# Conv states, samples' B and C, and the second shift's rows turned in a few wide flips; a page buffer and a job order changed with them

## The chip, the cores and the metric

One core of one Trainium2 chip runs the whole program. The metric is the device time of one execution in microseconds (us). The kernel before was timed three times. A difference of about 0.5% is the least that such a measurement tells from none.

## The reference, cut to what matters

The program is one layer of a decode step for a prompt of 256 tokens (blocks of 128) and 8 samples of one token each, all in float32:

```
mod = silu(c) @ w_mod + b_mod               # c: 8 samples and 1 prompt; six parts, shift2 among them
h   = rms_norm(x) * (1 + scale1) + shift1
q, k, v, f, z, xBC, dt, gA, gB = split(h @ w_in)
oA  = forgetting attention                  # samples: 2 cached pages of 128 keys and values each
xa  = concat(conv_state, xBC)               # 3 old columns of 3072 channels ahead of the new ones
conv_new = xa[last 3]                       # an output, for the samples and for the prompt
xs, B, C = split(silu(conv4(xa)))
y   = SSD scan of the prompt in 2 chunks of 128; samples: one state update of 32 x 64 x 128 each
x  += gate1 * (merge of both branches @ w_o)
h2  = rms_norm(x) * (1 + scale2) + shift2
x  += gate2 * moe(h2)                       # 16 experts, top 2 inside one of 4 groups
```

conv_new is written row by row of 3072 channels: 3 rows for each of the 8 samples and 3 for the prompt. The samples' B and C are wanted as rows in a scratch array, from which they are spread over partitions. The router's logits and the tokens' rows of h2 both need shift2.

## The kernel before, in words

The kernel is written in hand-placed instructions with semaphores. Channels lie on partitions ("turned" tensors, 128 channels by 264 tokens), weights come from HBM through a ring of six slots of 1 MB, and TensorE (PE) turns tiles with `flip`, a product with the identity (line 1704). One list, `jobs`, gives the order of the work. Every engine walks it and does its own part of each job: PE fills a PSUM bank, ACT or DVE read it out. The seven banks go round in the order of the list, so a job waits until the job seven banks before it has been read.

The jobs that the text names:

- `xbc i` (24 of them) are the channel blocks of xBC. DVE (L1387 to L1395) puts the old columns ahead, copies the last three columns of each sample and of the prompt into `tails[:, i, 27]`, and sums the convolution. ACT applies SiLU (L924, L925) into `u`.
- `sk b q` turn the samples' key pages, `ss` multiplies queries by keys (L1862 to L1870) and ends in the semaphore `ss_done`, `sm` and `sp` are the softmax and its turning (L1012, L1013 on ACT).
- `so h` (L1888) multiplies probabilities and value pages of samples 4h to 4h+3, `sx h` turns the result and DVE copies it into `att_T` (L1412, 8 copies).
- POOL issues the page loads (L798), key pages first, into the four page buffers `kvr`. For value pages of samples 4 to 7 it waits until `so 0` has left those buffers.
- `ct i`, six jobs, turn `tails` four blocks at a time (27 rows of 512 channels). ACT copies each to SBUF (L1021) and issues two stores (L1022, L1024).
- `bs 0`, `bs 1` turn the samples' columns of the eight B and C blocks (8 flips to 8 rows). ACT copies them (L1027), stores them and the samples' x and decays to scratch (L1031 to L1035) and loads d_skip, spread over partitions (L1036).
- `bt` and `xs a g` turn B and x of the prompt (DVE multiplies xs by dt, L1420), `cb a` is C times B (L1424 masks it), `ab a b` spreads the sums of decays, DVE subtracts (L1439), ACT takes exp (L1049), DVE multiplies by cb (L1222, `weigh`), and `y a b` (L1945, L1948) is the scan's product. POOL scales xs (L805, L812) for the chunk's state and, in the second chunk, C (L823).
- `z i`, 16 jobs of 128 channels, come between these. The list `fill` says where.
- `fs`, the sample states (`ssm`; ACT L1079, DVE L1471 to L1480, loads and stores by POOL L829, L844), the gates `g` and the products `pa` follow, then `yn` (L2026), `sw`, `pb 0` to `pb 7` (L2035), the output product `o` (L2043) and the experts (L2127, L2152, L2181).
- `sw` makes shift2 @ w_router: 8 products with the prompt's column spread over 128 columns, 8 with the samples' 8 columns, and the bias twice (L1965 to L1970). `shr 0` to `shr 3`, after `pb 3`, turn the differences of the samples' shift2 from the prompt's, and the prompt's shift2 itself, one block of 128 channels at a time (16 flips).

SP issues the weights in the order of first use. It waits for the job that last used a slot, and for nothing that is changed here. The loads wait in one queue.

Before its first L1439 DVE waits for the scratch stores and for d_skip, and makes two copies of it (L1434):

```
if a == 0 and b == 0:
    dve.wait_ge(bs_out, 80)
    for q in range(2):
        r = slice(64 * q, 64 * q + 64)
        link(v.tensor_copy(dsk[r, :], dskf[r, q:SH:2]))
```

## Time and profile before

| what | value |
|---|---|
| runs | 774.11, 774.36, 777.66 us; median 774.36 |
| the profiled execution | 773.63 us |
| its span | 772.0 us |
| PE busy | 730.3 us, 95% of the span |
| PEld (weight loads) | 500.8 us, 65% |
| DVE busy | 377.9 us, 49% |
| ACT busy | 291.7 us, 38% |
| POOL busy | 97.8 us, 13% |
| DMA | 219.47 MB, mean 284 GB/s |
| the chain that ended last | 70% PE, 8% DMA, 7% DVE, 6% ACT, 4% issue |

The table is read so. The span is what the profiler saw between the first and the last instruction, and the execution's own time is 1.63 us more. PE, PEld and the others are shares of the span and overlap. An idle PE is what an edit off PE can give back, some 42 us in all. "Issue" in the chain is time in which the engine waited for nothing that the profile shows.

### The profile page before, as it was taken

The numbers are of one execution on the slowest core, as the hardware profiler recorded it, in microseconds if no ns is written. First come the engines' busy times: TensorE is split into PE (matmuls) and PEld (weight loads), VectorE is DVE, ScalarE is ACT, GpSimd is POOL, SyncE is SP. The second block draws the span as 40 slices with busy tenths as digits, with TensorE's granted clock in tenths as the row PEclk, the third lists the DMA queues.
The fourth block names the chain that finished last, engine by engine and source line by source line (L and its number), as shares of the span: only waits on it lengthen the run. The fifth ranks groups of instructions, "written<-read, shape, count | busy, mean of one in ns | idle before, by whom it ended". The sixth has DMA issues, their size and how long they took to land.

```text
span 772.0 us, 12380 instructions
## 1 busy us (share of the span) xinstructions
PE 730.3 (95%) x4469; PEld 500.8 (65%) x4469; DVE 377.9 (49%) x952; ACT 291.7 (38%) x686; POOL 97.8 (13%) x169
## 2 busy tenths in 40 slices
PE   3899998999999989999989999999999999999986
PEld 3475687778785667888877888887634344434433
DVE  1364337777674087587999311112513244324423
ACT  3221157656775223667876001012522122212202
POOL 4331021122110113430111000000010000000000
PEclk9999999999999999999999999999999999999998
DMA  9997374979785621349999797467999999999991
GB/s 313 330 346 226 115 205 153 327 234 321 243 296 176 216 60 60 117 124 367 378 292 336 257 345 272 146 265 294 338 420 422 415 423 422 417 421 421 418 383 60
DMA packets 88649, 219.47 MB, mean 284 GB/s; under 512 B 11990, under 2 KB 55598, under 8 KB 75145
## 3 DMA queue, kind: packets, MB, share of 16 engines
q1 hardware_dynamic: 73360, 181.71, 64.3%
q0 software_dynamic: 7840, 31.67, 12.1%
q10 hardware_dynamic: 7384, 5.25, 2.2%
q8 instruction: 38, 0.62, 0.3%
q14 instruction: 27, 0.21, 0.1%
HBM read 207.07 MB, written 13.22 MB: 285 GB/s over the span
## 4 chain that ended last, share of the span: by engine, by line
PE 70%; DMA 8%; DVE 7%; ACT 6%; issue 4%; SPq 1%; ACTq 1%; POOLq 1%; POOL 0%; DVEq 0%
PE bank L1794 16%; PE bank L2127 13%; PE bank L2035 7%; PE bank L2152 6%; PE bank L2043 4%; PE bank L1704 4%; PE bank L1787 3%; PE bank L2017 3%; DMA conv_out<-in_w_mod 3%; DMA arena<-in_w_up 3%; PE bank L2181 2%; PE bank L1744 2%; DMA arena<-in_state_ssm 2%; DVE arena L1471 1%; ACT arena L1079 1%
## 5 line engine op out<-in xcount | busy, mean ns | idle before, releaser
L1794 PE MATMUL bank<-h_normed,weight_ring 128*128 128x264 f32 x1024 | 237.4, 388 | 2.2 <-ACT conv_work L1087 2.2
L1794 PEld LDWEIGHTS bank<-h_normed,weight_ring 128*128 128x128 f32 x1024 | 191.2, 190 | 37.3 <-issue 4.2
L2127 PE MATMUL bank<-arena,h_normed 128*64 128x512 f32 x136 | 60.3, 594 | 0.0
L2035 PE MATMUL bank<-y_T,weight_ring 128*128 128x264 f32 x256 | 57.4, 386 | 0.4 <-DVE y_T L1508 0.4
L2035 PEld LDWEIGHTS bank<-y_T,weight_ring 128*128 128x128 f32 x256 | 48.5, 190 | 8.7 <-issue 0.5
L1592 DVE TENSOR_TENSOR arena<-arena,bank 128x512 f32<-128x512 f32 x8 | 8.4, 1052 | 85.6 <-PE bank L2127 85.6
L1704 PE MATMUL bank<-identity,arena 128*128 128x128 f32 (+5 forms) x218 | 30.6, 281 | 13.4 <-ACT arena L903 9.5
L1079 ACT ACTIVATE arena<-conv_out,early_small 128x128 f32<-128x128 f32 x128 | 38.3, 387 | 11.3 <-DVE arena L1471 10.2
L2152 PE MATMUL bank<-arena 128*64 128x512 f32 x88 | 39.2, 595 | 0.0
L1395 DVE SCALAR_TENSOR_TENSOR conv_work<-conv_work,conv_out 128x288 f32<-128x288 f32 x72 | 37.8, 525 | 2.5
L872 POOL DMA_INDIRECT h_normed<-h_scratch,token_rows x7 | 7.1, 1018 | 248.7 <-DVE token_rows L1559 135.1
L2127 PE MATMUL bank<-conv_out,h_normed 128*64 128x512 f32 x76 | 34.7, 594 | 2.6 <-DMA arena<-in_w_up 2.5
L1704 PEld LDWEIGHTS bank<-identity,arena 128*128 128x128 f32 (+5 forms) x218 | 26.1, 149 | 17.1 <-issue 11.2
L1133 ACT ACTIVATE h_normed<-bank,conv_tails 128x128 f32<-128x128 f32 x64 | 17.4, 383 | 51.4 <-PE bank L1704 47.9
L2127 PE MATMUL bank<-weight_ring,h_normed 128*64 128x512 f32 x112 | 31.7, 592 | 0.0
L2017 PE MATMUL bank<-att_T,weight_ring 128*128 128x264 f32 x128 | 28.9, 387 | 1.6 <-ACT arena L1085 1.6
L1787 PE MATMUL bank<-h_normed,weight_ring 128*64 128x264 f32 x256 | 29.8, 388 | 0.0
L2043 PE MATMUL bank<-arena,weight_ring 128*128 128x264 f32 x128 | 29.4, 388 | 0.0
L1517 DVE TENSOR_TENSOR arena<-arena,bank 128x264 f32<-128x264 f32 x8 | 3.4, 430 | 51.9 <-PE bank L2035 51.9
L2127 PEld LDWEIGHTS bank<-arena,h_normed 128*64 128x64 f32 x136 | 18.3, 137 | 16.0 <-issue 16.0
L2017 PEld LDWEIGHTS bank<-att_T,weight_ring 128*128 128x128 f32 x128 | 24.2, 190 | 6.1 <-ACT arena L1085 2.0
L1599 DVE SCALAR_TENSOR_TENSOR x_residual<-bank,conv_out,x_residual 128x256 f32<-128x256 f32 x56 | 26.3, 477 | 3.2 <-PE bank L2181 2.7
(407 smaller groups left out, 1227.8 us busy)
## 6 DMA issues: line engine op xcount, KB each, us to landing
weight_ring<-in_w_in SPq DMA_DIRECT2D x36, 1024.0 KB, 6.2
weight_ring<-in_w_mod SPq DMA_DIRECT2D x22, 1024.0 KB, 9.7
arena<-in_w_down SPq DMA_DIRECT2D x11, 1024.0 KB, 23.8
arena<-in_w_gate SPq DMA_DIRECT2D x10, 1024.0 KB, 14.0
weight_ring<-in_w_down SPq DMA_DIRECT2D x10, 1024.0 KB, 14.7
weight_ring<-in_w_up SPq DMA_DIRECT2D x9, 1024.0 KB, 25.0
arena<-in_state_ssm POOLq DMA_DIRECT2D x8, 1024.0 KB, 11.3
out_ssm_sample<-arena POOLq DMA_DIRECT2D x8, 1024.0 KB, 8.8
```

What stands on the lines that cost most here:

```text
L1079: ins = fn(bx[:, NST * c:NST * c + NST], bc[:, b, 0, :], ACT.Copy, scale=xdt[:, c, b:b + 1])
L1133: ins = fn(xg[:, c, :], banks[5 + h][:, 128 * q:128 * q + 128], ACT.Identity, bias=shq[:, c:c + 1])
L1395: link(v.scalar_tensor_tensor(acc, x[:, w:w + XO], vec[:, 104 + 24 * w + i:105 + 24 * w + i], acc, ALU.mult, ALU.add), conv_ready if w == ...
L1599: v.scalar_tensor_tensor(xT[:, c, 0:NP], comb_bank(c)[:, 0:NP], modT[:, 40 + c, NS:NC], xT[:, c, 0:NP], ALU.mult, ALU.add)
L1704: return tr(out, x, ident[0:k, 0:k])
L1787: ins = mm(ps[64 * x:64 * x + 64, 0:T], slot(s)[:, c, o:o + HD], hT[:, c, :], start=c == 0, stop=c == KD - 1, tile_position=(0, 64 * x))
L1794: ins = mm(ps[:, 0:T], w, hT[:, c, :], start=c == 0, stop=c == KD - 1)
L2017: ins = mm(ps[:, 0:T], w, attT[:, c, :], start=c == 0, stop=c == KD - 1)
L2035: ins = mm(ps[:, 0:T], w, yT[:, c, :], start=c == 0, stop=c == NXB - 1)
L2043: ins = mm(ps[:, 0:T], slot(s)[:, c, 128 * (i % 2):128 * (i % 2) + 128], gT[:, c, :], start=c == 0, stop=c == KD - 1)
L2127: ins = mm(banks[i][BLK * e:BLK * e + BLK, :], xg[:, 4 * h + c, BLK * e:BLK * e + BLK], ws[e][c], start=h == 0 and c == 0, stop=h == 1 and ...
L2152: ins = mm(banks[2 + q][BLK * e:BLK * e + BLK, :], aT[:, 2 * h + c, BLK * e:BLK * e + BLK], ws[e][c][:, 512 * q:512 * q + 512], start=h == ...
```

## The change

- The buffer `tails` is laid out as `[128, 6, 27, 4]`: blocks c, c+6, c+12 and c+18 lie beside each other, so that one flip turns 108 columns. `ct` becomes two jobs, of 4 and of 2 flips; four stores take the place of twelve.
- SiLU of the samples' B and C goes to a place of its own (`samples_bc`, 64 columns), which one flip turns: `bs` is one job, put right after `modt 5`.
- The load of d_skip moves to the front of the program (ACT), its copies to DVE's part of `ft`. The router bias gets zeros under it on 128 partitions (one memset on POOL), and its load follows a wait for `consts`. `head_in` counts one load more.
- The value pages of samples 4 to 7 go to a buffer of their own, `kvh`, in the space of the sample queries and turned keys. POOL waits for `ss_done` in place of `so 0`, and PE's `so 1` for the new semaphore `kvh_full`. `so 1` also has its own output buffer.
- `sw` multiplies 72 columns of modT, 16 outputs each, in 8 products and one for the bias. DVE takes the samples' rows and row 8; a job `sb` spreads row 8 over 128 partitions with one product.
- `shr` is one flip of 72 columns, stored to scratch by one DMA. The samples' rows and the prompt's are loaded back from there (two loads in ACT's part of `o 0`), and `rk` waits for these.
- The order between `modt 5` and the scan, and `fill`, are new.

The diff, cut to its core:

```diff
-        tails = sb("conv_tails", [128, NCB, 27])
+        tails = sb("conv_tails", [128, NCB // 4, 27, 4])
...
             if c == 7:
-                jobs += [("sm",), ("mod", 5), ("ct", 0), ("sp",), ("modt", 5)]
+                jobs += [("sm",), ("mod", 5), ("ct", 0), ("sp",), ("modt", 5), ("bs",)]
...
-        jobs += [("so", 0), ("ct", 1), ("sx", 0)] + [("z", i) for i in range(4)] + [("so", 1), ("ct", 2), ("sx", 1)]
-        jobs += [("bs", 0), ("bs", 1)]
-        jobs += [("bt", a) for a in range(2)]
+        jobs += [("z", 0), ("so", 0), ("z", 1), ("sx", 0), ("ct", 1), ("z", 2)] + [("bt", a) for a in range(2)]
+        jobs += [("so", 1), ("z", 3), ("sx", 1)]
         fill = {(0, 1): [("z", 4)], (0, 3): [("z", 5)], 
-                (0, 5): [("z", 6)], (0, 6): [("ct", 3)], (0, 7): [("z", 7)], (1, 0): [("z", 8), ("zs", 0)],
-                (1, 1): [("z", 9)], (1, 2): [("z", 10)], (1, 3): [("z", 11), ("ct", 4), ("zs", 1)], (1, 4): [("z", 12)],
-                (1, 5): [("z", 13), ("zs", 2)], (1, 6): [("z", 14), ("ct", 5)], (1, 7): [("z", 15), ("zs", 3)]}
+                (0, 5): [("z", 6)], (0, 7): [("z", 7)], (1, 0): [("z", 8), ("zs", 0)],
+                (1, 1): [("z", 9)], (1, 2): [("z", 10)], (1, 3): [("z", 11), ("zs", 1)], (1, 4): [("z", 12)],
+                (1, 5): [("z", 13), ("zs", 2)], (1, 6): [("z", 14)], (1, 7): [("z", 15), ("zs", 3)]}
...
-        jobs += [("pb", i) for i in range(4)] + [("shr", i) for i in range(4)] + [("pb", i) for i in range(4, 8)]
+        jobs += [("pb", i) for i in range(4)] + [("shr",), ("sb",)] + [("pb", i) for i in range(4, 8)]
...
-                    if kind == 1 or b >= 4:
-                        bk, use = bank_of[("sk", b - 4, 1) if kind == 0 else ("sk", b + 4, 1) if b < 4 else ("so", 0)]
+                    if kind == 1 and b >= 4:
+                        pool.wait_ge(ss_done, 1)
+                    elif kind == 1 or b >= 4:
+                        bk, use = bank_of[("sk", b - 4, 1) if kind == 0 else ("sk", b + 4, 1)]
                         pool.wait_ge(bank_filled[bk], use)
+                    home = kvh if kind == 1 and b >= 4 else kvr
...
-            act.dma_start(brow[:], t["b_router"].rearrange("(o d) -> o d", o=1)).then_inc(head_in, 16)
+            act.wait_ge(consts, 3)
+            act.dma_start(brow[0:1, :], t["b_router"].rearrange("(o d) -> o d", o=1)).then_inc(head_in, 16)
+            act.dma_start(dskf, t["d_skip"].to_broadcast([128, SH])).then_inc(head_in, 16)
...
-                    link(v.tensor_copy(tails[:, i, 0:24].rearrange("p (b w) -> p b w", w=3), xs4[:, :, 1:4]))
-                    link(v.tensor_copy(tails[:, i, 24:27], x[:, NP:NP + 3]))
+                    tail = tails[:, i % (NCB // 4), :, i // (NCB // 4)]
+                    link(v.tensor_copy(tail[:, 0:24].rearrange("p (b w) -> p b w", w=3), xs4[:, :, 1:4]))
+                    link(v.tensor_copy(tail[:, 24:27], x[:, NP:NP + 3]))
...
                     if a == 0 and b == 0:
-                        dve.wait_ge(bs_out, 80)
-                        for q in range(2):
-                            r = slice(64 * q, 64 * q + 64)
-                            link(v.tensor_copy(dsk[r, :], dskf[r, q:SH:2]))
+                        dve.wait_ge(bs_out, 64)
...
                 elif k == "ct":
                     pe.wait_ge(conv_ready, NCB)
-                    for q in range(4):
-                        ins = flip(ps[0:27, 128 * q:128 * q + 128], tails[:, 4 * j[1] + q, :])
+                    for q in range(4 if j[1] == 0 else 2):
+                        ins = flip(ps[0:4 * 27, 128 * q:128 * q + 128],
+                                   tails[:, 4 * j[1] + q].rearrange("p s q -> p (s q)"))
                 elif k == "bs":
                     pe.wait_ge(u_ready, NCB)
-                    for q in range(4):
-                        ins = flip(ps[0:NS, 128 * q:128 * q + 128], u[:, NXB + 4 * j[1] + q, NP:T])
+                    ins = flip(ps[0:2 * SG * NS, 0:128], samples_bc)
...
                     for c in range(KD):
-                        mm(ps[:, 0:NE], modT[:, 24 + c, NS:NC].to_broadcast([128, 128]), wr[:, c, :],
-                           start=c == 0, stop=False)
-                    mm(ps[:, 0:NE], onesf[0:1, :], brow[:], start=False, stop=True)
-                    for c in range(KD):
-                        mm(ps[0:NS, NE:2 * NE], modT[:, 24 + c, 0:NS], wr[:, c, :], start=c == 0, stop=False)
-                    ins = mm(ps[0:NS, NE:2 * NE], onesf[0:1, 0:NS], brow[:], start=False, stop=True)
+                        mm(ps[0:NC * KD, 0:NE], modT[:, 24 + c:32 + c, :], wr[:, c, :], start=c == 0, stop=False)
+                    ins = mm(ps[0:NC * KD, 0:NE], onesf[:, 0:NC * KD], brow[:], start=False, stop=True)
                 elif k == "shr":
                     pe.wait_ge(shdiff_ready, 1)
-                    for q in range(4):
...
+                    ins = flip(ps[0:NC * KD, 0:128], shifts)
+                elif k == "sb":
+                    read_out(pe, ("sw",))
+                    ins = mm(ps[:, 0:NE], ident[:, NS:NC].to_broadcast([128, 128]), shift9, start=True, stop=True)
...
-                    pe.wait_ge(shdiff_rows, 2)
+                    pe.wait_ge(shq_in, 32)
```

## Rows read from the trace of the kernel before

**Rows 1.** Busy time by stretch: stretch, PE, PEld, DVE, ACT, POOL, PEclk, DMA share, GB/s

```profile
241.50:281.00 39.50, 33.42 (x216) 24.14 (x218) 12.51 (x38) 9.98 (x25) 7.92 (x9) 1.00 0.56 167
281.00:299.70 18.70, 18.70 (x147) 14.95 (x143) 16.63 (x47) 5.80 (x15) 0.00 (x0) 1.00 0.30 90
344.50:403.00 58.50, 57.15 (x290) 49.62 (x288) 52.92 (x62) 47.03 (x121) 8.43 (x16) 1.00 1.03 342
```

**Rows 2.** Timeline of PE, so 0 to the first y: start, length, line, tiles, [idle before]

```profile
244.54 2.92 PE L1888 MATMUL bank<-arena 128*32 128x512 f32 x24 [1.33 <-issue]
...
248.78 14.41 PE L1794 MATMUL bank<-h_normed,weight_ring 128*128 128x264 f32 x64
264.05 2.92 PE L1888 MATMUL bank<-arena 128*32 128x512 f32 x24 [0.87 <-DMA arena<-in_cache_v]
...
268.29 3.66 PE L1704 MATMUL bank<-identity,conv_out 128*8 128x128 f32 x32
...
274.16 0.61 PE L1931 MATMUL bank<-cums_in_parts,head_pick 96*128 96x128 bf16 x8 [1.32 <-ACT arena L1038]
...
280.69 0.66 PE L1945 MATMUL bank<-arena 128*64 128x128 f32 x8 [1.86 <-issue]
```

**Rows 3.** Timeline of DVE, sx 1 to the first weigh

```profile
268.56 1.46 DVE L1412 COPY att_T<-bank 64x8 f32<-64x8 f32 x8 [18.05 <-PE bank L1704]
270.73 2.87 DVE L1420 TENSOR_TENSOR arena<-bank,early_small 128x512 f32<-128x512 f32 x4 [0.71 <-DVE att_T L1412]
...
275.32 2.22 DVE L1434 COPY early_small<-arena 64x16 f32<-64x16 f32 x2 [1.00 <-DMA arena<-in_d_skip]
277.58 2.29 DVE L1439 TENSOR_SCALAR arena<-bank,early_small 128x128 f32<-128x128 f32 x8
279.90 0.69 DVE L1222 TENSOR_TENSOR arena<-arena 128x512 f32<-128x512 f32 x1
```

**Rows 4.** The line of the two copies: ns min/median/max of one, first and last start

```profile
L1434 DVE COPY early_small<-arena x2: 174/1092/2010, 275.3 to 277.4; 64x16 f32<-64x16 f32 x2
```

**Rows 5.** Timeline of POOL, first and last of 8 value pages, then the first scaling

```profile
248.89 0.54 POOL L798 DMA_DIRECT2D arena<-in_cache_v  x1 [19.36 <-issue]
...
259.84 0.54 POOL L798 DMA_DIRECT2D arena<-in_cache_v  x1 [1.33 <-issue]
273.68 3.62 POOL L805 TENSOR_TENSOR arena<-arena,early_small 128x2048 f32<-128x2048 f32 x1 [13.31 <-DVE arena L1420]
```

**Rows 6.** Timeline of all engines, POOL's second scaling and DVE beside it

```profile
305.86 3.62 POOL L812 TENSOR_TENSOR arena<-arena,early_small 128x2048 f32<-128x2048 f32 x1
...
307.87 1.13 DVE L1439 TENSOR_SCALAR arena<-bank,early_small 128x128 f32<-128x128 f32 x4 [1.49 <-ACT arena L1047]
309.03 1.00 DVE L1222 TENSOR_TENSOR arena<-arena 128x512 f32<-128x512 f32 x1
```

**Rows 7.** Timeline of PE, sw and the first pb

```profile
445.07 1.94 PE L1965 MATMUL bank<-conv_out 128*128 128x16 f32 x16
...
448.36 0.91 PE L2035 MATMUL bank<-y_T,weight_ring 128*128 128x264 f32 x3 [0.41 <-DVE y_T L1508]
```

**Rows 8.** The chain that ended last, at shr: start, length, what

```profile
477.08 1.75 PE bank L1704 x16
```

**Rows 9.** The start of the program: PE's timeline, ACT's queue, and the chain

```profile
13.16 4.72 PE L1704 MATMUL bank<-identity,arena 128*128 128x128 f32 x26 [2.70 <-DMA arena<-in_x_sample]
...
33.47 0.66 PE L1704 MATMUL bank<-identity,arena 96*128 96x96 f32 x6
...
13.95 0.30 ACTq L911 DMA_DIRECT2D router_bias<-in_b_router  x1
...
7.33 24.11 DMA conv_out<-in_w_mod
```

**Rows 10.** Waits of PE in the experts: waited for, us in total, times, longest

```profile
PE bank L2127 <- DMA arena<-in_w_up: 2.5, 2, 1.3
```

**Rows 11.** Timeline of PE, gates after a wait, in the stretch of the sample states

```profile
403.84 10.95 PE L1794 MATMUL bank<-h_normed,weight_ring 128*128 128x264 f32 x48 [2.20 <-ACT conv_work L1087]
```

More of the change, by code:

```diff
@@ L113, in build @@
         exo = early[:, 1761:2033]
-        dsk = exo[:, 0:NXB]
+        dskf, dsk = more[:, 0:SH], more[:, SH:SH + NXB]
+        samples_bc = more[:, SH + NXB:SH + NXB + 2 * SG * NS]
         x2, xdt = (exo[:, NXB + 128 * i:NXB + 128 * i + 128].rearrange("p (l b) -> p l b", b=NS) for i in range(2))
@@ L151, in build @@
         pnb = part(NS)
-        bias = [part(768).rearrange("p (h k) -> p h k", h=2),
+        bias_lo = part(768)
+        otoks = (otok, bias_lo[:, 0:KVW])
+        bias = [bias_lo.rearrange("p (h k) -> p h k", h=2),
                 work[:, 0:768].rearrange("p (h k) -> p h k", h=2)]
@@ L716, in _ @@
             link(g.memset(epsc[:], EPS))
+            link(g.memset(brow[:], 0.0))
             link(g.memset(blk, 0.0))
@@ L924, in conv_silu @@
                 link(fn(u[:, i, 0:NP], cacc[:, i % 2, 0:NP], ACT.Silu))
-                link(fn(u[:, i, NP:T], cacc[:, i % 2, NP + 3:XO:4], ACT.Silu), u_ready)
+                link(fn(u[:, i, NP:T] if i < NXB else samples_bc[:, NS * (i - NXB):NS * (i - NXB) + NS],
+                        cacc[:, i % 2, NP + 3:XO:4], ACT.Silu), u_ready)
             act.wait_ge(x_in, 48)
@@ L951, in _ @@
                     link(fn(fdw[:, 0, :], fd[:], ACT.Abs))
-                    act.wait_ge(head_in, 16 * 10)
+                    act.wait_ge(head_in, 16 * 11)
                     link(fn(hcol[0:SH, 1:2], hcol[0:SH, 1:2], ACT.Exp))
@@ L1024, in _ @@
[L1024 to L1036 removed]
+                    i, cols = j[1], slice(512 * j[1], min(512 * j[1] + 512, CD // 4))
@@ new lines, in _ @@
+                    release(act, fn(ctok[:, cols], ps[0:4 * 27, 0:cols.stop - cols.start], ACT.Copy), j)
+                    act.dma_start(t["conv_sample"].rearrange("o b w (q c) -> (o b w q) c", q=4)[:, cols],
+                                  ctok[0:96, cols]).then_inc(o_tail, 16)
+                    act.dma_start(t["conv_prompt"].rearrange("o b w (q c) -> (o b w q) c", q=4)[:, cols],
+                                  ctok[96:108, cols]).then_inc(o_tail, 16)
+                elif k == "bs":
+                    release(act, fn(bcT, ps[0:2 * SG * NS, 0:NST], ACT.Copy), j)
+                    for q in range(2):
+                        act.dma_start(bc_d.rearrange("g (b k n) -> k g b n", b=NS, k=2)[q],
+                                      bcT[SG * NS * q:SG * NS * q + SG * NS, :]).then_inc(bs_out, 16)
+                    act.wait_ge(u_ready, NCB)
+                    act.dma_start(sx_d.rearrange("(c p) b -> p c b", p=128), u[:, 0:NXB, NP:T]).then_inc(bs_out, 16)
+                    act.wait_ge(fd_sp, 1)
+                    act.dma_start(se_d, ex[:]).then_inc(bs_out, 16)
@@ L1296, in _ @@
                     ps = filled(dve, j)
-                    dve.wait_ge(head_in, 16 * 10)
+                    dve.wait_ge(head_in, 16 * 11)
                     w0, w1, w2 = fdw[:, 0, :], fdw[:, 1, :], fdw[:, 2, :]
@@ L1342, in _ @@
                     dve.wait_ge(consts, 4)
+                    for q in range(2):
+                        r = slice(64 * q, 64 * q + 64)
+                        link(v.tensor_copy(dsk[r, :], dskf[r, q:SH:2]))
                     link(v.tensor_tensor(lfn[0:NS, :].rearrange("p (b h) -> p b h", b=NS),
@@ L1430, in _ @@
                     if a == 0 and b == 0:
-                        dve.wait_ge(bs_out, 80)
-                        for q in range(2):
-                            r = slice(64 * q, 64 * q + 64)
-                            link(v.tensor_copy(dsk[r, :], dskf[r, q:SH:2]))
+                        dve.wait_ge(bs_out, 64)
                     for i in range(4):
@@ L1761, in _ @@
                 elif k == "cst":
-                    pe.wait_ge(head_in, 16 * 10)
+                    pe.wait_ge(head_in, 16 * 11)
                     for q in range(3):
@@ L1885, in _ @@
                             c = 16 * (4 * hf + bb)
-                            w, x = ((psT[:, q, c:c + 32], kvr[:, bb, q, :]) if q < NPG else
+                            w, x = ((psT[:, q, c:c + 32], (kvr, kvh)[hf][:, bb, q, :]) if q < NPG else
                                     (pn[0:NS, c:c + 32], vtok[0:NS, 2, :]))
```

91 lines of the change are left out of this document (38 added, 53 removed).

## The prediction

> **What bounds the kernel now.** I read the busy shares first, then the busy times by stretch, then PE's own timeline, and last what the other engines do where PE is idle. PE is busy 95% of the span and the chain that ended last is 70% PE, so an edit pays where it takes instructions off PE or closes one of its gaps. The stretch where most of the change lies, from the end of modt 5 to the scan, is the worst used one: 33.42 of 39.50 us, while in the first chunk's scan PE is never idle [rows 1]. Its gaps are four: 1.33 before so 0 (it waits until ACT has read sp), 0.87 before so 1 (the value pages), 1.32 before the first ab (ACT's read-out of bt) and 1.86 before the first y [rows 2]. The last isn't PE's own. DVE stood 1.00 for the load of d_skip and then took 2.22 for two copies of it [rows 3], of which one took 2.01 and the other 0.17 [rows 4].
>
> **The stretch before the scan.** I rebuild it from the durations of the rows. PE ends modt 5 at 244.54 - 1.33 = 243.2 [rows 2]. Prices: a z is 14.41 / 4 = 3.6, a so 2.9, a flip 3.66 / 32 = 0.11, an ab pair 0.55 [rows 2]. The new order is bs (one flip) 0.1, z 0 to 246.9, so 0 to 249.8, z 1 to 253.4, sx 0 and ct 1 (6 flips) to 254.1, z 2 to 257.7, bt (8 flips) to 258.6, so 1 to 261.5, z 3 to 265.1, sx 1 to 265.6. The read-outs of sp and of both so fall under a z, so the first gap is closed, and so is the one before ab.
>
> The pages: eight loads go out one after another, the last 259.84 - 248.89 = 11.0 after the first, and the first 1.5 after so 0 ended (244.54 + 2.92 = 247.46) [rows 2, 5]. The so 1 that waited for them began at 264.05, 4.2 after the last issue. From ss_done, which comes before sp and thus some 6 us before modt 5 ends (237), the last is out at 249.5 and landed by 253.7. PE wants them at 258.6, with 5 us to spare. Behind that wait on POOL stand only these loads and the scaling of xs, which comes later.
>
> From sx 1 on DVE leads: 8 copies 1.46 to 267.1, four xs 2.87 to 270.0 [rows 3]. POOL then starts its scaling, 3.62, and ends at 273.7 [rows 5]. The wait for d_skip and both copies are gone from here. DVE masks cb in 0.7 (a tile of weigh's size, which took 0.69) and does 8 decays in 2.29 [rows 3], to 273.0, and comes to weigh. Here the rows show a hold: the copy of 2.01 ended with POOL's scaling (273.68 + 3.62 = 277.3), and a weigh met by POOL's second scaling took 1.00 in place of 0.69 [rows 3 to 6]. The decays took 1.13 for four while POOL was scaling, as without it (2.29 for eight). So weigh waits until 273.7 and ends at 274.4, and y 0 starts at 274.5. It started at 280.69 [rows 2]: **6.2 us** less. PE alone would be ready at 265.6 + 16 flips 1.8 + cb 0.9 (8 products as long as flips) + ab 0.5 + z 4 3.6 + ab 0.5 = 272.9, so a gap of 1.6 is left before y, caused by DVE and POOL.
>
> The Trainium skill ("SBUF — State Buffer", section "Who interferes with whom") says that a VectorE instruction with both inputs in SBUF shares a read port with a GpSimd instruction that reads SBUF and that the later one is fully blocked, while one with a single SBUF input outside the two-port modes isn't. The weigh of 1.00 and the decays of 1.13 agree with it. Without that rule one would let weigh start at 273.0, and the sum would be 0.7 larger.
>
> **The three ct in fill.** The jobs at (0, 6), (1, 3) and (1, 6) go, 12 flips of 0.11: **1.3 us**, since PE has no gap there [rows 1, 2]. What could be late next is DVE, 16.63 of 18.70 busy in the first chunk [rows 1]; 2.1 of slack cover the 0.4 that leave it.
>
> **sw, shr, sb.** Before, sw's 16 wide products took 1.94, 0.12 each, and then PE stood 0.41 for DVE's last step of yn [rows 7]. The 18 new products cost 0.5 us at least (a quarter of that pace, for narrower weights) and 2.2 at most. Either way they end before 448.36, when yn lets pb 0 go, so their saving is **nothing**: the 0.41 grows to at most 3. shr was 1.75 [rows 8]; after it is one flip, 0.11, and sb two passes of 0.12: **1.4 us** less, in the middle of pb where nothing else is waited for. The way of the rows through scratch, two loads in o 0, has all of the rest of o to land; one more issue on ACT, some 0.4, comes before x is updated.
>
> **At nothing.** At the start: the bias's load behind a wait that is over by then, one more issue (0.3 like its neighbour at 13.95 [rows 9]) ahead of ACT's squares, under the mod 1 products; if that cover isn't there, 0.3. The load of d_skip must land before PE's flips of the conv states at 33.47, for they wait for head_in. It leaves at 14.3. The nearest rows: x had landed 13.2 into the span, a load of weights took 24.1 [rows 9]. So it lands between 27.5 and 38.4, which is 0 or 4.9 us of cost. I take 0, as a small load in ACT's queue is nearer to x; 4.9 is kept for the range. The two copies in DVE's ft: 0.35 to 2.2, under a q job of PE. The tail copies in steps of four: as many elements, as strided as those of sx, 0.18 each [rows 3]: 0. ACT loses four read-outs and eight issues, SP's queue keeps its order, and z 0's weights are asked for when xbc 21 ends, long before 243.
>
> **Sum.** 6.2 + 1.3 + 1.4 = 8.9 us. What follows moves as a whole: the states' loads are issued after the last y and after fs, the ring's by the jobs that free it, and the experts' loads after yn and pb 7. So even where the DMA is the limit (PE waits 2.5 us for w_up late in the experts [rows 10]) it starts earlier by as much. The profiled execution, 773.63, becomes 764.7. It lies 0.73 under the median of 774.36, so I forecast 765.5 for the median.
>
> **The rivals.**
> - A, as summed: 765.5, own range 763.5 to 767.5. For it: every term is a duration of a row, and the gap's causes are named in it. Chance 0.66.
> - B, DVE and POOL keep the scan's pace: the decays too are held by POOL's scaling. Then they start at 273.7, y at 273.7 + 2.3 + 0.7 + 0.1 = 276.8, 3.9 gained in place of 6.2, and the 0.4 of the first chunk's ct is lost to DVE. 774.36 - 6.2 = 768.2. Against: 1.13 for four beside POOL [rows 6]. Chance 0.15.
> - C, the stretch of the sample states keeps its end. The DMA is full there, share 1.03, PE lacks 1.35 us, and ACT made it wait 2.20 after it [rows 1, 11]. If an absolute rate of transfers rather than their start sets that end, 7.5 are lost, and only shr's 1.4 stays: 773.0. Against: in the chunks before, the share is 0.30, so nothing is carried over into it. Chance 0.08.
> - D, slower. The pause before pb 0 grows from 0.41 to between 1 and 3, and TensorE's clock falls from 2.4 to 1.2 GHz after it. At half clock a product of 0.22 takes 0.45. The change ends over 0.5% slower once this costs more than 8.9 + 3.9 = 12.8, that is from 57 of the 128 products of pb 0 to 3 on. With 64 of them at half clock 765.5 + 14.4 = 779.9. Against: after a pause of 2.20 the 48 products took 10.95, 0.23 each, at full clock [rows 11]. Chance 0.04.
> - E, an early start that isn't early. Either d_skip lands at 38.4 (4.9 lost), or the pages aren't there sooner than before, 264.05, and so 1 stands from 258.6 on, 5 lost: 770.5. Chance 0.07.
>
> **How the numbers follow.** About 0.5%, 3.9 us, is the least that a measurement of this kernel tells from no change, so "faster" is below 770.5. That holds A, B and half of E: 0.84. "Same" is C and the rest of E, 0.12. "Slower" is D, 0.04. The range 763.0 to 770.6 takes in A with the 0.7 of weigh and 1 us for the gap of 1.6 below it, B and E. It leaves out C and D, 0.12, and some of A's edges.
>
> **What would show it.** In the profile after: so 0 and so 1 without a wait, and ab too; the first y at 274.5 of the span, with PE idle some 1.6 before it, weigh ending with or after POOL's scaling; no flips of conv_tails after that; PE idle 1 to 3 us before pb 0, with the clock at 1.00; 0.35 between pb 3 and pb 4. I am wrong if the first y comes after 276, if a gap stands before the conv states' flips at 33.5, if the 7.5 us won by the end of fs are fewer at the first pb, or if a clock under 1 shows.

## The result and the profile after

The median of six runs is 766.32 us (765.52 to 767.11), of six of the kernel before 774.24 (772.95 to 779.24). The ratio is 0.9901, with the 95% interval 0.9882 to 0.9920. Forecast were 765.5 and "faster"; the range 763.0 to 770.6 holds the time, and the whole interval lies beyond the 0.5% that the prediction called the least change to be told from none. Measured in two more groups (again, again2 below), the same kernel came to ratios of 0.9952 (interval 0.9931 to 0.9972, so not clearly beyond 0.5%) and 0.9919: the gain of the medians was 7.9, 4.9 and 6.6 us. The profiled execution took 767.11 us, with a span of 765.5 against 772.0.

Where the 6.5 us between the two spans come from is read by stretch. The columns are those of [rows 1]. Of before, from the end of modt 5 to the first y, to the update of the states, to sw, to o, to the experts, to the end:

```profile
243.20:280.70 37.50, 31.50 (x202) 23.08 (x202) 11.78 (x35) 8.71 (x22) 7.92 (x9) 1.00 0.58 175
280.70:344.50 63.80, 63.80 (x461) 51.14 (x461) 46.61 (x117) 34.74 (x66) 20.06 (x15) 1.00 0.30 93
344.50:444.90 100.40, 96.65 (x466) 83.08 (x465) 81.57 (x95) 61.94 (x164) 12.29 (x22) 1.00 0.97 323
444.90:507.30 62.40, 61.99 (x312) 53.00 (x312) 8.41 (x26) 3.92 (x6) 0.83 (x4) 1.00 0.66 236
507.30:554.10 46.80, 46.55 (x279) 36.50 (x277) 15.43 (x69) 14.41 (x33) 0.00 (x0) 1.00 0.88 337
554.10:772.00 217.90, 205.59 (x1085) 86.71 (x1085) 75.51 (x235) 48.32 (x118) 7.12 (x7) 0.99 0.93 381
```

The same six of after:

```profile
244.00:275.90 31.90, 29.94 (x191) 21.68 (x189) 10.07 (x33) 7.40 (x21) 6.25 (x6) 1.00 0.60 195
275.90:338.40 62.50, 62.50 (x449) 49.98 (x449) 47.63 (x119) 34.20 (x62) 20.06 (x15) 1.00 0.30 93
338.40:438.70 100.30, 98.23 (x466) 84.21 (x466) 81.17 (x95) 60.37 (x163) 12.29 (x22) 0.98 0.96 322
438.70:501.20 62.50, 60.54 (x281) 51.54 (x280) 8.88 (x29) 1.84 (x3) 0.83 (x4) 0.97 0.66 237
501.20:549.60 48.40, 48.24 (x281) 38.16 (x279) 15.43 (x69) 14.48 (x33) 0.00 (x0) 0.96 0.85 327
549.60:765.50 215.90, 205.55 (x1085) 86.71 (x1085) 75.49 (x235) 48.32 (x118) 7.13 (x7) 1.00 0.93 384
```

Ahead of them the start took 0.8 us longer: the first products on x began 0.86 later (they waited for its load), and the 64 products of mod behind them took 5.43 for 3.66, why no run says. In again, the same kernel, these began 0.16 later and took 3.66, so it isn't the change. The stretch to the first y won 5.6, the chunks 1.3, the sample states nothing. From sw to o the stretch is as long as before, though it does 31 products fewer; the experts' routing lost 1.6; the last stretch won 2.0. The column of the clock tells what the busy shares hide: 0.98, 0.97 and 0.96 where before had 1.00.

**The stretch before the scan**, PE's timeline of after, beside [rows 2]:

```profile
244.11 3.73 PE L1806 MATMUL bank<-h_normed,weight_ring 128*128 128x264 f32 x16
247.77 2.92 PE L1902 MATMUL bank<-arena 128*32 128x512 f32 x24
250.62 3.83 PE L1806 MATMUL bank<-h_normed,weight_ring 128*128 128x264 f32 x16
254.75 0.63 PE L1716 MATMUL bank<-identity,arena 128*128 128x128 f32 x4 [0.30 <-ACT arena L1028]
...
259.96 1.92 PE L1902 MATMUL bank<-y_T,arena 128*32 128x512 f32 x16
...
273.61 0.61 PE L1945 MATMUL bank<-cums_in_parts,head_pick 96*128 96x128 bf16 x8
275.88 0.66 PE L1959 MATMUL bank<-arena 128*64 128x128 f32 x8 [1.66 <-issue]
```

so 0, so 1 and ab wait for nothing; of the four gaps one is left, and a new small one stands before sx 0. DVE and POOL, beside [rows 3] and [rows 5]:

```profile
267.17 1.45 DVE L1422 COPY att_T<-bank 64x8 f32<-64x8 f32 x8 [10.24 <-ACT z_samples L1069]
268.66 2.87 DVE L1430 TENSOR_TENSOR arena<-bank,early_small 128x512 f32<-128x512 f32 x4
...
272.29 2.29 DVE L1446 TENSOR_SCALAR arena<-bank,early_small 128x128 f32<-128x128 f32 x8
274.61 1.17 DVE L1228 TENSOR_TENSOR arena<-arena 128x512 f32<-128x512 f32 x1
```

```profile
239.39 0.54 POOL L807 DMA_DIRECT2D y_T<-in_cache_v  x1 [8.99 <-issue]
...
250.28 0.54 POOL L807 DMA_DIRECT2D y_T<-in_cache_v  x1 [1.27 <-issue]
271.61 3.62 POOL L814 TENSOR_TENSOR arena<-arena,early_small 128x2048 f32<-128x2048 f32 x1 [20.79 <-DVE arena L1430]
```

The chain is the one forecast: eight copies, four xs, then the decays beside POOL's scaling, and a weigh of 1.17 in place of 0.69 that ends 0.55 after POOL (275.23).

The gap before sx 0 comes from ACT's queue: its timeline of after shows an issue that lasts 6.05 us, so that z 0, ready at 247.8, was read at 253.5, and so 0 behind it.

```profile
246.87 0.44 ACTq L1042 DMA_DIRECT2D sx_scratch<-conv_out  x1
247.34 6.05 ACTq L1044 DMA_DIRECT2D se_scratch<-expand_in  x1
253.52 0.39 ACT L1068 ACTIVATE weight_ring<-bank 128x256 f32<-128x256 f32 x1 [7.52 <-issue]
```

**sw, shr and sb**, PE's timeline of after, beside [rows 7] and [rows 8]:

```profile
438.83 1.19 PE L1979 MATMUL bank<-conv_out 128*72 128x16 f32 x16
439.87 0.28 PE L1980 MATMUL bank<-router_bias,ones 128*72 128x16 f32 x2
442.11 30.41 PE L2043 MATMUL bank<-y_T,weight_ring 128*128 128x264 f32 x128 [1.96 <-DVE y_T L1515]
472.35 0.27 PE L1716 MATMUL bank<-identity,conv_tails 128*72 128x128 f32 x1
472.46 0.29 PE L1986 MATMUL bank<-conv_tails,identity 128*128 128x16 f32 x2
472.61 3.58 PE L2043 MATMUL bank<-y_T,weight_ring 128*128 128x264 f32 x15
```

The next pb starts 0.26 after shr, where before shr took 1.75: 1.5 won. But pb 0 to 3 took 30.41 in place of 28.72 (the row of before, whole):

```profile
448.36 28.72 PE L2035 MATMUL bank<-y_T,weight_ring 128*128 128x264 f32 x128 [0.41 <-DVE y_T L1508]
```

In slices of 4 us, the last number but two is the granted clock; in after, at pb 0 and at the gather of the experts' tokens:

```profile
440.00:444.00 4.00, 2.04 (x9) 1.55 (x8) 2.24 (x13) 0.64 (x2) 0.00 (x0) 0.82 1.02 333
444.00:448.00 4.00, 4.00 (x15) 3.30 (x14) 0.00 (x0) 0.00 (x0) 0.00 (x0) 0.75 1.09 387
540.00:544.00 4.00, 3.90 (x25) 3.32 (x25) 2.23 (x9) 2.84 (x4) 0.00 (x0) 0.70 0.90 293
544.00:548.00 4.00, 4.00 (x32) 3.88 (x31) 1.78 (x9) 0.00 (x0) 0.00 (x0) 0.88 0.99 355
```

A mean between 0.5 and 1 is a clock that stood at its lower level (1.2 GHz) for part of the slice; such a stretch is called a dip below. The profiled execution of before shows no slice under 1.00 between 4 and 760 us. A third dip of after lies in the sample states, where the 48 products of [rows 11] take 1.69 more:

```profile
397.59 12.64 PE L1806 MATMUL bank<-h_normed,weight_ring 128*128 128x264 f32 x48 [2.07 <-ACT conv_work L1095]
```

### The profile page after: what moved, and what is told of

Same layout as the page of the kernel before. It is cut to its first block, busy times and chain, and to the rows that moved or that the text cites. A ratio compares the mean times of both kernels' runs of the same rounds, so it can differ in the third digit from the quotient of the medians.

```text
span 765.5 us, 12245 instructions
## 1 busy us (share of the span) xinstructions
PE 731.1 (96%) x4413; PEld 500.5 (65%) x4413; DVE 377.4 (49%) x955; ACT 286.4 (37%) x678; POOL 97.9 (13%) x170
## 4 chain that ended last, share of the span: by engine, by line
PE 66%; SPq 11%; DVE 7%; ACT 7%; DMA 4%; issue 2%; ACTq 2%; DVEq 0%
PE bank L1806 19%; SPq L602 8%; PE bank L2043 8%; PE bank L2135 6%; PE bank L1716 4%; PE bank L2051 4%; PE bank L2025 4%; PE bank L2160 4%; SPq L600 3%; PE bank L1799 3%; PE bank L1756 3%; DMA arena<-in_w_up 3%; DMA arena<-in_x_sample 1%; DVE arena L1478 1%; PE bank L1959 1%
## 5 line engine op out<-in xcount | busy, mean ns | idle before, releaser
L1806 PE MATMUL bank<-h_normed,weight_ring 128*128 128x264 f32 x1024 | 239.8, 390 | 2.1 <-ACT conv_work L1095 2.1
L2043 PE MATMUL bank<-y_T,weight_ring 128*128 128x264 f32 x256 | 59.1, 395 | 2.0 <-DVE y_T L1515 2.0
L2051 PEld LDWEIGHTS bank<-arena,weight_ring 128*128 128x128 f32 x128 | 24.1, 190 | 5.2 <-issue 1.3
```

The source lines that it names most:

```text
L1806: ins = mm(ps[:, 0:T], w, hT[:, c, :], start=c == 0, stop=c == KD - 1)
L2043: ins = mm(ps[:, 0:T], w, yT[:, c, :], start=c == 0, stop=c == NXB - 1)
L2051: ins = mm(ps[:, 0:T], slot(s)[:, c, 128 * (i % 2):128 * (i % 2) + 128], gT[:, c, :], start=c == 0, stop=c == KD - 1)
```

## The experiments

All edits are to the kernel after. The first table gives the times, in groups that shared a chip and its runs of the kernel before.

| kernel | median, us (range, runs) | before, us | ratio to before [interval] |
|---|---|---|---|
| again (after, unchanged) | 768.33 (766.03 to 773.01, 12) | 773.27 | 0.9952 [0.9931, 0.9972] |
| fill | 765.38 (763.25 to 766.15, 6) | 773.27 | 0.9896 [0.9872, 0.9920] |
| order | 765.71 (763.01 to 766.80, 6) | 773.27 | 0.9898 [0.9872, 0.9925] |
| stores | 767.09 (764.47 to 772.14, 12) | 773.27 | 0.9921 [0.9897, 0.9946] |
| pages | 778.44 (776.28 to 781.04, 5) | 773.81 | 1.0056 [1.0029, 1.0083] |
| dskip | 771.82 (768.99 to 776.12, 8) | 773.81 | 0.9977 [0.9954, 1.0001] |
| ct | 767.62 (765.35 to 773.21, 10) | 773.81 | 0.9942 [0.9917, 0.9968] |
| flips | 767.30 (766.84 to 768.91, 4) | 773.81 | 0.9925 [0.9905, 0.9944] |
| again2 (after, unchanged) | 767.11 (765.01 to 770.90, 6) | 773.73 | 0.9919 [0.9891, 0.9946] |
| best | 764.23 (762.03 to 764.48, 5) | 773.73 | 0.9861 [0.9833, 0.9888] |
| latepool | 766.68 (765.38 to 767.27, 4) | 773.73 | 0.9900 [0.9868, 0.9931] |
| flips2 | 767.35 (765.62 to 768.89, 5) | 772.06 | 0.9932 [0.9904, 0.9961] |

The second gives what PE's timeline of each profiled execution shows, in us.

| kernel | z 0 to first y | wait before pb 0 | pb 0 to 3 | 32 gather products | span |
|---|---|---|---|---|---|
| before | (another order) | 0.41 | 28.72 | 3.84 | 772.0 |
| after | 31.77 | 1.96 | 30.41 | 5.25 | 765.5 |
| again | 32.31 | 1.97 | 30.30 | 4.71 | 764.4 |
| fill | 32.05 | 0.19 | 28.72 | 5.46 | 764.3 |
| order | 30.84 | 1.97 | 30.41 | 5.47 | 763.7 |
| stores | 31.29 | 1.97 | 30.15 | 4.63 | 762.9 |
| pages | 43.35 | 1.96 | 30.41 | 5.31 | 779.1 |
| dskip | 34.72 | 1.97 | 28.72 | 5.21 | 767.4 |
| ct | 32.26 | 1.97 | 28.72 | 5.18 | 764.5 |
| flips | 32.27 | 1.96 | 30.41 | 3.84 | 765.6 |
| again2 | 32.19 | 1.96 | 28.72 | 5.31 | 763.4 |
| best | 29.71 | 0.19 | 28.72 | 4.71 | 762.5 |
| latepool | 31.29 | 1.96 | 30.40 | 4.82 | 765.3 |
| flips2 | 31.94 | 0.19 | 28.72 | 4.68 | 764.7 |

**again and again2** are the kernel after once more, as the base of their groups.

> The changed kernel again, as the measure for the others of this call: 765.5 to 767.1 us. Two theories of why it missed the sum (766.3 for 765.5): (1) TensorE's clock dips to its lower level after the two pauses of 2 us, before the gates' last part and before pb 0, which cost 1.7 us each in the profile of the changed kernel; if the clock is a matter of the run and not of the kernel, this profile can show pb 0 to 3 in 28.7 us after the same pause, and the time is then near 765.5. (2) the dips belong to the pauses: then pb 0 to 3 take 30.4 again.

> The kernel after, unchanged, as the base for the two beside it: it gave 766.3 and 768.3 as medians, with mean clocks of 0.986 to 0.996 between executions. I expect 767 with a spread of 765.5 to 773, the lowest times at the highest clocks, about 0.7 us for each 0.001 of the mean clock.

What a single chip's group says is thus good to some 2 us between medians: 768.33, 767.11 and, in the first group, 766.32 are one kernel. Its mean granted clock ran from 0.986 to 0.996 in again's executions, with the highest times at the lowest clocks (772.77 and 773.01 us at 0.986). So the small effects below are read in the stretches of the profiles first.

**fill: is it the pause that slows pb 0?** Four wide products that nobody reads go ahead of sw's own.

```diff
                     pe.wait_ge(head_in, 16 * 11)
+                    for _ in range(4):
+                        mm(ps[:, 64:320], xT[:, 0, 0:128], xT[:, 1, 0:256], start=True, stop=True)
```

> Four idle-time products of 256 columns (8 passes, about 1.8 us) are put into sw ahead of its own, into columns nobody reads. The products of sw then end at 441.9 in place of 440.1, and yn lets pb 0 go at 442.1 as before. If the pause brings the dip of the clock: no dip at pb 0, pb 0 to 3 take 28.7 in place of 30.4, and the program ends 1.7 us sooner if PE sets the end, less if the experts' loads do. If the dip is chance or comes from something else: no change, 766.3, dips in some profiles all the same.

```profile
438.04 1.97 PE L1979 MATMUL bank<-x_residual 128*128 128x256 f32 x8
439.85 1.16 PE L1981 MATMUL bank<-conv_out 128*72 128x16 f32 x16
...
441.33 2.02 PE L2045 MATMUL bank<-y_T,weight_ring 128*128 128x264 f32 x8 [0.19 <-DVE y_T L1515]
```

pb 0 starts no sooner, since it waits for yn, but the 128 products take 28.72. The median is 2.95 below again's, more than the stretch shows, but order's, without these products, is 2.62 below it too: the medians don't size the effect. Over all profiles: with a wait of 1.96 or 1.97 pb 0 to 3 took 28.72 three times (dskip, ct, again2) and 30.15 to 30.41 seven times; with 0.19 or 0.41 it took 28.72 all four times. After the long pause the dip came in most executions, not in all, and after the short one it didn't come. That the pause is a condition of it rests on these four executions. Its length alone doesn't decide: ahead of the 48 products of the sample states PE pauses in every kernel, and the dip followed pauses of 1.96 to 2.17 (seven executions) and 2.62 (pages), but not those of 1.73 (ct), 2.20 (before), 2.22, 2.27, 2.59 and 2.61 (best, stores, dskip, again2). What else decides stays open. So sw's products were worth nothing in the prediction's sense and cost up to 1.7 by being gone.

**order: does PE's order in the stretch hold back the scan?** so 1 goes ahead of bt and sx 1 ahead of z 3.

```diff
-        jobs += [("z", 0), ("so", 0), ("z", 1), ("sx", 0), ("ct", 1), ("z", 2)] + [("bt", a) for a in range(2)]
-        jobs += [("so", 1), ("z", 3), ("sx", 1)]
+        jobs += [("z", 0), ("so", 0), ("z", 1), ("sx", 0), ("ct", 1), ("z", 2), ("so", 1)]
+        jobs += [("bt", a) for a in range(2)] + [("sx", 1), ("z", 3)]
```

> so 1 moves ahead of bt, and sx 1 ahead of z 3, so that DVE makes its 8 copies of sx 1 (1.45 us) under z 3 and starts on xs when PE has turned them, not 1.5 us later. My theory is that DVE's chain, sx copies, xs, POOL's scaling, weigh, sets the first y: it should start 1.5 us sooner (274.3 of 275.9 in the span), PE idle 0.2 before it, and the total falls by 1.5 (764.8 of 766.3). If PE or the value pages set it (rival): so 1 now waits for pages, which landed at 256, before 259, so no; or nothing moves, 766.3.

From z 0 to the first y it takes 30.84, 1.4 less than the middle of the other kernels (32.2), and PE's idle before y falls to 0.60. Of the 1.4, 1.07 is this idle time (1.67 before) and the rest a shorter wait before sx 0 (0.45). DVE's copies of sx 1 begin at 262.56 instead of 267.17, counted from z 0 3.4 sooner, but xs then waits for PE's flips, at 266.55. The gain is near the 1.5 expected and not the 3.4 that the copies moved: PE is next in the row.

**stores: what held ACT's issue for 6 us?** The small store goes ahead of the large one.

```diff
+                    act.wait_ge(fd_sp, 1)
+                    act.dma_start(se_d, ex[:]).then_inc(bs_out, 16)
                     act.wait_ge(u_ready, NCB)
                     act.dma_start(sx_d.rearrange("(c p) b -> p c b", p=128), u[:, 0:NXB, NP:T]).then_inc(bs_out, 16)
-                    act.wait_ge(fd_sp, 1)
-                    act.dma_start(se_d, ex[:]).then_inc(bs_out, 16)
```

> In bs the small store of the decays is issued ahead of the store of the samples' x. ACT's issue of it took 6.05 us in the changed kernel (0.94 before), and z 0 and so 0 were read out late, which cost PE 0.30 before sx 0. If the issue was held by the descriptors of the x store ahead of it (64 KB in runs of 32 bytes): the issues now take under 2 us together, z 0 is read at 247.9 and the 0.30 is gone, total 766.0. If the hold comes from the page loads and weights in flight at the time: one of the two issues still takes 5 us or more.

```profile
244.98 0.43 ACTq L1042 DMA_DIRECT2D se_scratch<-expand_in  x1
245.45 0.44 ACTq L1044 DMA_DIRECT2D sx_scratch<-conv_out  x1
246.01 0.38 ACT L1068 ACTIVATE weight_ring<-bank 128x256 f32<-128x256 f32 x1 [2.00 <-PE bank L1806]
```

The issues take 0.43 and 0.44 and z 0 is read as soon as PE is done. The issue was held by what stood ahead of it in ACT's queue, the store of 64 KB in runs of 32 bytes (eight samples of a row), and not by its own size (2.1 KB). That isn't the whole condition: in before the two stores stood in the same order, and the second issue took 0.94. There the mean busy share of the DMA engines was 0.38 (270.9 to 272.4), in after 1.07 (247.3 to 253.4). It isn't the page loads either: in pages these go out only later, and the issue took 4.69. That the traffic makes the difference is not shown. The wait before sx 0 is gone, which is worth 0.9 in the stretch.

**pages: what is the value pages' own place and semaphore worth?** POOL waits for so 0 again before it asks for the last eight pages, in place of `ss_done` (the end of the samples' scores, which the expectation names wrongly).

```diff
-                        pool.wait_ge(ss_done, 1)
+                        bk, use = bank_of[("so", 0)]
+                        pool.wait_ge(bank_filled[bk], use)
```

> Edit to the kernel after: POOL waits for so 0 again, in place of the sample states' last decay, before it asks for the last eight value pages; nothing else is changed. My theory: the pages are then the last thing so 1 waits for. so 0 ended at 250.68 in the run after, the first load leaves 1.5 later (252.2), the eighth 11.0 after that (263.2), and so 1 starts some 4.2 after the eighth, at 267.4, instead of 259.96: PE stands 7.4 before so 1, and the first y comes 6 to 7.5 later, at 282 to 283. Time 766.3 + 6.8 = 773.1 (ratio to before 0.998). Rival: the semaphore of its own matters little, as z 3, sx 1 and the DVE work behind them give back half: y at 279, time 769.5.

```profile
267.11 3.64 PE L1903 MATMUL bank<-y_T,arena 128*32 128x512 f32 x16 [6.54 <-DMA y_T<-in_cache_v]
270.68 1.93 PE L1903 MATMUL bank<-arena 8*32 8x512 f32 x8
272.54 6.70 PE L1807 MATMUL bank<-h_normed,weight_ring 128*128 128x264 f32 x16
```

The wait is as forecast, but after it so 1 takes 5.6 for 3.0 and z 3 6.70 for 3.83: the clock was at its lower level. 6.54 + 2.6 + 2.9 = 12.0, less the small wait before sx 0, which is gone here, is about the 11.1 that the stretch grew by. The expectation costed the wait alone; here the stall cost nearly twice its length. With it the whole change ends 0.6% slower than the kernel before (interval 0.3 to 0.8). The new order needs the early pages.

**dskip: does the place of the copies matter, once the load is early?**

```diff
-                    for q in range(2):
-                        r = slice(64 * q, 64 * q + 64)
-                        link(v.tensor_copy(dsk[r, :], dskf[r, q:SH:2]))
...
                     if a == 0 and b == 0:
                         dve.wait_ge(bs_out, 64)
+                        for q in range(2):
+                            r = slice(64 * q, 64 * q + 64)
+                            link(v.tensor_copy(dsk[r, :], dskf[r, q:SH:2]))
```

> Edit to the kernel after: the two copies of d_skip stand again where they did, behind bt and the decays and ahead of weigh; the load stays at the front, so it has long landed. Theory of the held copy: the pure wait for the load is gone, the first copy meets POOL's scaling and is held until it ends (275.2 in the run after), 0.17 for the second, then weigh 0.69: y 0.2 to 1.0 later than after, at 276.1 to 276.9 (by stretch, modt 5's end to y: 32.0 to 32.8 against 31.8). Rival, the copies cost 2.2 wherever they stand: y at 278.1. In the prediction's terms: nearly all of the gain of 6.2 would belong to the order of the jobs and the early load, none to the place of the copies. Time 766.3 + 0.5 = 766.8 by the first, 768.5 by the rival.

```profile
271.29 3.18 DVE L1441 COPY more_places<-more_places 64x16 f32<-64x16 f32 x2
274.51 2.29 DVE L1446 TENSOR_SCALAR arena<-bank,early_small 128x128 f32<-128x128 f32 x8
276.83 0.69 DVE L1228 TENSOR_TENSOR arena<-arena 128x512 f32<-128x512 f32 x1
```

The text of the expectation has the copies behind the decays; the kernel has them ahead of these, where they were before, and that decides. POOL scaled from 270.62 to 274.24. The first copy was held until then, and the decays, which POOL doesn't hold, now stand behind a held instruction: y comes 2.5 later, by the rival's price. The copies' place is 2.5 of the stretch's gain. The delay has a price behind it, too. PE stood 4.40 before the first y, and the products after it ran slow:

```profile
277.62 1.12 PE L1959 MATMUL bank<-arena 128*64 128x128 f32 x8 [4.40 <-issue]
278.68 4.80 PE L1806 MATMUL bank<-h_normed,weight_ring 128*128 128x264 f32 x16
```

In after the same two took 0.66 and 3.83, so this dip cost 1.43 (the granted clock was 0.66 from 276 to 280). The 2.53 and the 1.43 are the 4.0 by which the span is longer than again2's (767.4 for 763.4), and the median is 4.1 above the mean of again's and again2's (767.72). The profiled execution is the fastest of the eight; the others' mean clocks were 0.984 to 0.992, and what slowed these beyond it wasn't profiled.

**ct: do the twelve flips in the chunks reach the end?** The conv states are turned as before, in six jobs of four flips, with the old layout of the tails and twelve stores. Its diff is the change's own for `tails` and `ct`, reversed, of which the order's part is:

```diff
-        jobs += [("so", 1), ("z", 3), ("sx", 1)]
+        jobs += [("so", 1), ("z", 3), ("ct", 2), ("sx", 1)]
...
-                (0, 5): [("z", 6)], (0, 7): [("z", 7)], (1, 0): [("z", 8), ("zs", 0)],
+                (0, 5): [("z", 6)], (0, 6): [("ct", 3)], (0, 7): [("z", 7)], (1, 0): [("z", 8), ("zs", 0)],
```

with ct 4 at (1, 3) and ct 5 at (1, 6).

> Edit to the kernel after: the conv states' turns go as in the kernel before, six jobs of four narrow flips with read-outs and two stores each (four of the six in the places they had), and the copies of the tails write the old layout. Everything else as after. Theory of the sum: 18 flips of 0.11 come back, 2.0 us, of which 12 flips, 1.3, in the chunks (first y to fs 63.8 instead of 62.5) and 0.4 in the stretch before the scan, where DVE and POOL set the first y, so that costs 0.0 to 0.4: time 766.3 + 1.3 to 1.7 = 767.6 to 768.0. Rival: the chunks have room for them (DVE sets their pace) and the time doesn't change; the 1.3 that the first y to fs gained would then come from something else.

From the first y (275.02) to the states' update (338.83) it takes 63.81, to the hundredth what it took before, against 62.50 in after. The sum's term is right. The median, 767.62, lies where the first theory had it, but it can't be told from again2's by itself.

**flips and flips2: does PE time saved in pb reach the end?** The single flip of the shifts is made 16 times; in flips2 the four products of fill stand ahead of pb 0 too.

```diff
-                    ins = flip(ps[0:NC * KD, 0:128], shifts)
+                    for _ in range(16):
+                        ins = flip(ps[0:NC * KD, 0:128], shifts)
```

> Edit to the kernel after: the one flip of the shifts in pb is made 16 times, as many as the kernel before had; the result is the same. Theory that PE's time in pb reaches the end whole: shr 1.75 again instead of 0.27, pb to experts 1.5 longer, time 766.3 + 1.5 = 767.8. Rival: the end is partly set by the experts' loads (their issues stand in the chain that ended last of the run after), so a part of it is taken up by waits of PE in the experts, and the time grows by 0 to 0.7: then shr's term of the sum was worth less than its PE time.

> Edit to the kernel after: the 16 flips of the shifts as in the run flips, and the four wide products ahead of pb 0 as in the run fill. Asked: the 32 products of the experts' gather took 3.84 in the profiles of before and of flips, the two kernels with 16 flips in pb, and 5.2 to 5.5 in all eleven without. If that is tied to the flips: 3.84 again, o to the experts 47.0, and then removing the flips gained 1.5 and lost 1.4, net nothing, and the time is that of fill, 765.4 (764.5 to 766). If it is chance: about 5.2 again, o to the experts 48.3 to 48.6, and the time is fill's plus the flips' 1.6, 767.0. By both, pb 0 to 3 takes 28.7 after a pause of 0.2.

From pb 0 to o flips takes 60.69 and after 59.06: 1.63 of PE time for the 1.5 expected. It reaches the experts, too: from their first product to the end of the span all the kernels of this study need 215.9 to 217.0, wherever that product lies (546.3 in best, 562.8 in pages), so the experts' loads don't set an absolute end. In flips the time didn't grow by all of it: its ratio is 0.9925 and again2's 0.9919. In the profiled execution the gather of the experts' tokens ran at 3.84 as before; in after it took 5.25:

```profile
541.99 5.25 PE L2107 MATMUL bank<-conv_states,conv_out 128*128 128x128 f32 x32
```

flips2 was to say whether the two are tied. They aren't: with the 16 flips it is 4.68, and its median is fill's plus 1.97 (on another chip; by the ratios, 0.9932 for 0.9896, it is 2.8). Beside flips, though, flips2's four products gained nothing in the medians (0.9932 for 0.9925), though its pb 0 to 3 took 28.72 and those of flips 30.41. (The expectation gives 5.2 to 5.5 for the eleven kernels without the flips; the table has 4.63 to 5.47.)

**latepool: is it POOL that makes the first weigh long?** POOL's first scaling also waits until DVE has weighed twice.

```diff
                 read_out(pool, ("xs", a, 3))
+                if a == 0:
+                    pool.wait_ge(w_ready, 2)
```

> Edit to the kernel after: POOL's first scaling of xs waits until DVE has weighed twice. Theory of the held read: the first weigh takes 0.69 instead of 1.17, y starts 0.5 sooner, and the scaling, now at 275.5 to 279.5, holds a later weigh or two for up to 2.5 us (a weigh of 2 to 3 us in DVE's rows) while the single-input decays keep 1.13 for four. Rival, 1.17 belongs to the first weigh of a chunk whoever runs beside it (its pipeline, its semaphore): then it stays 1.17 and no later weigh is longer than 0.75. The time is 766 to 769 either way.

DVE's and POOL's timelines of latepool:

```profile
273.89 0.69 DVE L1230 TENSOR_TENSOR arena<-arena 128x512 f32<-128x512 f32 x1
...
276.51 1.12 DVE L1448 TENSOR_SCALAR arena<-bank,early_small 128x128 f32<-128x128 f32 x4
277.67 3.13 DVE L1230 TENSOR_TENSOR arena<-arena 128x512 f32<-128x512 f32 x1
```

```profile
276.63 3.62 POOL L816 TENSOR_TENSOR arena<-arena,early_small 128x2048 f32<-128x2048 f32 x1 [26.49 <-DVE arena L1230]
```

The first weigh is 0.69, and the third, begun beside the scaling, takes 3.13 and ends 0.55 after it (280.25), just as the one of 1.17 did in after. The four decays inside the scaling keep 1.12. So the hold is shown by moving it. The Trainium skill ("SBUF — State Buffer", section "Who interferes with whom") states that a VectorE instruction with both inputs in SBUF waits for a GpSimd instruction that reads SBUF and was first, and the trace agrees with 1.17 and 3.13 in place of 0.69. Here moving it pays 0.5 at the first y and gives it back as a wait of 0.66 before a later one.

**best: the edits together**, fill, order, stores and latepool. (The store that goes ahead of the large one is that of the decays, as in stores; the expectation calls it that of the shift rows.)

> Edit to the kernel after: three earlier edits together. The store of the samples' x goes behind the store of the shift rows, so 1 before bt and sx 1 before z 3, and four wide products that nobody reads fill the pause ahead of pb 0; POOL's first scaling also waits for the second weigh, as in the run beside this one. If the gains add: y 1.1 (order) + 0.7 to 1.2 (stores) earlier from z 0 on, 28.7 instead of 30.3 for pb 0 to 3, so 767 - 1.0 - 0.9 - 1.6 = 763.5 (ratio to before 0.987). Rival: the first weigh can't start before the scan's data (xs, decays), so order and stores close the same gap, and the experts' loads set the end: 765.

From z 0 to the first y it takes 29.71, 2.5 less than again2, and pb 0 to 3 28.72. The median, 764.23, is 2.9 under again2's on the same chip and is the lowest of the study; its five runs, 762.03 to 764.48, all lie below again2's lowest of 765.01.

## Why the prediction was right, point by point

- **The stretch before the scan** was to give 6.2 and gave 5.6. From z 0 on I had 243.3 to 274.5, 31.2; the four executions of the unchanged kernel and of fill took 31.77 to 32.31. The wait before sx 0 (0.30 to 0.84) is most of the difference. The step that failed is "The read-outs of sp and of both so fall under a z": it put nothing for the stores that ACT issues between these read-outs, and the issue of one took 6.05, behind the large store. So 0 was read out later than a z covers. The rest held: the pages were landed in time, weigh ended with POOL's scaling, and PE's idle before y was 1.66 (forecast 1.6).
- **ct in fill**: 1.3 forecast, 1.31 measured, and undone by ct to the hundredth.
- **shr and sb**: 1.4 forecast, 1.5 measured. In the profiled execution the term was spent at once on the slower clock of pb 0 to 3 (1.69).
- **sw at nothing** is the term that was wrong in kind. I had put its products as covered by yn's end, and they are, but what they also did was keep PE busy. This is D's mechanism, in an eighth of the size that I priced (1.7 for 14.4): not 64 products at half clock but some 8 (1.69 / 0.22), and in seven of ten profiled executions rather than one of 25. My evidence against D was a single row, a pause of 2.20 with the clock at 1.00 after it [rows 11]; the same wait in after (2.07) was followed by 48 products in 12.64, not 10.95. One row where a thing didn't happen doesn't exclude it. By the prediction's own sign ("if a clock under 1 shows") this part of it was wrong.
- **What follows moves as a whole** held: the sample states took 100.3 for 100.4, which refutes C. That the dip of 1.69 in their gates cost nothing is due to ACT, which sets that stretch's end: the wait of 1.56 that stood before a later product is gone where the gates are slow (after, again, flips), and stands where they aren't (again2, stores, best).
- **B** is refuted by the eight decays of 2.29 that lie wholly inside POOL's scaling, and **E** by so 1 without a wait and by the conv states' flips without one.
- **At nothing**: the new load at the start and the copies in ft show no wait. (The conv states' flips began 1.4 later than before, at 34.91, behind the late x; in again they began at 33.37, so this isn't the load of d_skip.) Against the profile of before 1.4 to 1.6 were lost at the gather, which isn't in the sum; it appears in 12 of 13 profiled executions of changed kernels and not in the one of before. It is the clock again (0.70 in that slice), but I have no run that says what brings it there, and that stays open.
- The sum, 8.9, less 0.6 (the issue), 0.8 (the start), 1.7 (pb 0), 1.6 (the gather), plus 2.0 in the last stretch (0.6 of it the wait for w_gate, which fell from 0.73 to 0.15, and 1.4 behind PE's last product, where the output's stores land) makes the 6.5 of the spans within 0.3. The 1.4 at the very end is in no term of the sum, and no run ties it to the change. The medians differ by 7.9 here and by 4.9 and 6.6 in the groups of again and again2, all less than the 8.9 of the sum. That the forecast of 765.5 lies 0.8 from the median thus owes something to luck: in errors of both signs, and in the group that was measured.

## What to carry to other kernels

Before you take work off an engine "for nothing" because it only fills a wait, ask what the longer wait does to TensorE's clock: here the longer wait was followed by up to 1.7 us of slow products in seven of ten profiled executions, and with four products that nobody reads put back into it in none of three. When an order by hand is made tighter, price each DMA's issue by what stands ahead of it on that queue, put small stores ahead of large scattered ones, and keep read-outs that PE waits for off the queue that issues them. And look at what two engines on shared ports do at the same time: an instruction that is held also holds those behind it that wouldn't be.

## What the runs showed of the hardware that I had not expected

- An issue on ACT's queue lasted 6.05 us (4.69 to 6.60 in the changed kernels with this order of stores), though its own store is of 2.1 KB: it followed the issue of a 64 KB store in 32-byte runs. Turned round, the issues take 0.43 and 0.44. In before, with the same order of stores but the DMA engines less busy, it took 0.94.
- After a pause of 1.96 us the granted clock fell in seven of ten profiled executions, for a part of the next 8 us, at a cost of 1.4 to 1.7 us each time; after one of 4.40 the dip cost 1.43, and after one of 6.54 the clock stood at 0.50 for two slices of 4 us, which cost 5.5. An identical kernel had the dip behind a pause of 2.07 and none behind one of 2.61.
- The same kernel's mean clock differs between executions (0.986 to 0.996), and its times by up to 7 us with it. The kernel after, unchanged, had medians in three groups of 766.32, 768.33 and 767.11.
